# Attention scores of a pair of heads as products of 64 rows in the two row halves of TensorE, with the units' steps in the order of pairs

## The reference, cut to what matters

```python
ql = _rope(_rms_norm(_heads(q, A_HEADS), q_gain), cos, sin)       # A: full attention, 2 kv heads
s = jnp.einsum("bhgqd,bhkd->bhgqk", qi, k) * scale                # 64-wide contraction
p = jax.nn.softmax(s, axis=-1)
return jnp.einsum("bhgqk,bhkd->bhgqd", p, v)
# C: latent keys within +-128 tokens, a sink logit per head in the softmax
# D: all latent keys, a learned bias and a mask on them (4 kv heads)
```

## Time and profile before

| | us |
|---|---|
| median of 3 runs (2863.14 to 2866.6) | 2864.47 |
| the profiled execution | 2871.83 |
| its span in the trace | 2870.0 |
| TensorE busy, all of the span | 2591.3 (90%) |
| VectorE, ScalarE busy | 1084.9 (38%), 585.9 (20%) |

### The profile page before, as it was taken

The page is one execution under the profiler, slowest core; times in us unless marked ns, Lnnn a source line. Parts: engine busy times, 40 slices in busy tenths (PEclk is TensorE's granted clock), DMA queues, the critical chain, the costliest instruction groups (busy, mean ns, idle before and its releaser), DMA issues. The chain is left out here.

```text
span 2870.0 us, 44957 instructions
## 1 busy us (share of the span) xinstructions
PE 2591.3 (90%) x13801; PEld 1283.3 (45%) x13802; DVE 1084.9 (38%) x3199; ACT 585.9 (20%) x1378; POOL 387.1 (13%) x314
## 2 busy tenths in 40 slices
PE   6999989999899999999996588989998989899895
PEld 3566555645433333333332366666553333333331
DVE  3443351534333333333332643451452323233323
ACT  2222341411011111111111341331310111111111
POOL 0000001000021222222221200001001121112122
PEclk9999999999999999999998799999998999999997
DMA  7120303043588998999993402202336999998983
GB/s 272 57 92 30 118 16 136 10 180 125 224 276 305 348 326 281 321 326 327 337 369 101 166 2 91 89 29 103 128 143 252 381 402 387 384 390 277 390 332 110
DMA packets 104980, 619.29 MB, mean 216 GB/s; under 512 B 22832, under 2 KB 23088, under 8 KB 64688
## 3 DMA queue, kind: packets, MB, share of 16 engines
q1 hardware_dynamic: 71184, 530.30, 46.8%
q0 software_dynamic: 33696, 87.63, 12.5%
HBM read 578.84 MB, written 77.99 MB: 229 GB/s over the span
## 5 line engine op out<-in xcount | busy, mean ns | idle before, releaser
L1549 PE MATMUL ps<-wgu,xT 128*64 128x512 f32 x3584 | 808.4, 604 | 49.0 <-DMA wgu<-in_exp_gu 34.8
L1549 PEld LDWEIGHTS ps<-wgu,xT 128*64 128x64 f32 x3584 | 253.1, 139 | 509.2 <-issue 496.6
L1558 PE MATMUL ps<-wd,hiddenT 128*64 128x512 f32 x1824 | 419.5, 602 | 12.7 <-issue 12.2
L1478 POOL DMA_INDIRECT ffn_rows<-Y,six x114 | 182.6, 1602 | 1118.3 <-issue 654.7
L1726 DVE TENSOR_TENSOR hidden<-silu,ps 128x256 f32<-128x256 f32 x112 | 47.2, 421 | 703.9 <-ACT silu L1662 703.9
L659 PE MATMUL ps<-w_in,wgu 128*128 128x512 f32 (+3 forms) x768 | 268.7, 510 | 14.7 <-PEq L609 3.8
L1558 PEld LDWEIGHTS ps<-wd,hiddenT 128*64 128x64 f32 x1824 | 123.4, 137 | 228.3 <-issue 228.3
L659 PEld LDWEIGHTS ps<-w_in,wgu 128*128 128x128 f32 x768 | 151.1, 200 | 124.8 <-issue 111.4
L1662 ACT ACTIVATE silu<-ps 128x256 f32<-128x256 f32 x112 | 43.1, 384 | 800.1 <-PE ps L1549 800.1
L1657 ACT ACTIVATE Y<-ps,wc 128x512 f32<-128x512 f32 x114 | 78.4, 688 | 418.3 <-PE ps L1558 418.3
L1720 DVE TENSOR_SCALAR Y<-ps,wc 128x512 f32<-128x512 f32 x114 | 85.6, 751 | 199.4 <-PE ps L1558 199.4
(11 more groups left out here) (476 smaller groups left out, 2775.9 us busy)
## 6 DMA issues: line engine op xcount, KB each, us to landing
wgu<-in_exp_gu SPq DMA_DIRECT2D x128, 2048.0 KB, 13.9
wd<-in_exp_d SPq DMA_DIRECT2D x128, 1024.0 KB, 13.0
wgu<-in_ada_w SPq DMA_DIRECT2D x40, 1024.0 KB, 4.8
ada_start<-in_ada_w SPq DMA_DIRECT2D x8, 1024.0 KB, 8.0
w_in<-in_w_in SPq DMA_DIRECT2D x4, 2048.0 KB, 10.9
w_in<-in_w_out SPq DMA_DIRECT2D x4, 2048.0 KB, 12.5
wgu<-ffn_rows SPq DMA_DIRECT2D x16, 512.0 KB, 8.3
w_in<-in_w_in SPq DMA_DIRECT2D x2, 3072.0 KB, 14.3
```

The lines of the kernel that those rows point to most:

```text
L1478: pool.indirect_dma_start(out=v.acc_dram, out_offset=bass.IndirectOffsetOnAxis(ap=six[j][:, 0:1], axis=0), in_=Y[j][:, :], in_offset=None, ...
L1549: last = pe.matmul(ps[h * HB:(h + 1) * HB, 0, :], xT[:, k, h * HB:(h + 1) * HB], wgu[w[h]][:, k, :], start=(k == 0), stop=(k == KD - 1))
L1558: last = pe.matmul(ps[h * HB:(h + 1) * HB, 1 + c, :], G[:, f, h * HB:(h + 1) * HB], wd[w[h]][:, f, c * 512:(c + 1) * 512], start=(f == 0), ...
```

## The change

For A, C and D a new `pair_scores(w)` takes the place of `scores(u)`. It computes both units of a pair: for each, only the 64 partitions that hold its head (`rows`) of QT and KT, so the two units' products lie in the two row halves of the array and write to different PSUM buffers. The order is first unit's latent keys, second unit's, first unit's context keys, second unit's. The zeroed half of QT is no longer read, and its two memsets go. `pair_scores(w)` waits until both units of pair w - 1 have their exponentials (`s_exp.wait(pe, 2 * w)`), since both buffers are written again.

All three engines take their steps in pairs for A, C and D; B keeps the old order.

TensorE, the new function and the new order:

```diff
+                def pair_scores(w):
+
+                    s_exp.wait(pe, 2 * w)
+                    a = lo(2 * w)
+                    for c0, c1 in ((a, 512), (512, 768)):
+                        for u in (2 * w, 2 * w + 1) if c1 > c0 else ():
+                            s, q = units[u]
+                            rows = slice(s % 2 * HD, (s % 2 + 1) * HD)
+                            k0 = SEQ if c0 == 512 else key_tile(u, a // P) * P
+                            last = pe.matmul(pp[u % 2][:, c0:c1], QT[rows, s, q * P:(q + 1) * P], KT[rows, s // 2 if isD else 0, k0:k0 + c1 - c0],
+                                             start=True, stop=True)
+                            if c1 == 768:
+                                last.then_inc(s_sc.sem, 1)
...
+                else:
                     s_v.wait(pe, NT)
...
+                    pair_scores(0)
+                    for w in range(NU // 2):
+                        turn_probs(2 * w)
+                        if 2 * w + 2 < NU:
+                            pair_scores(w + 1)
+                        turn_probs(2 * w + 1)
+                        values(w)
```

ScalarE:

```diff
+                else:
+                    exps(1)
+                    for w in range(NU // 2):
+                        probs(2 * w)
+                        if w:
+                            inverse_rows(w - 1)
+                        probs(2 * w + 1)
+                        for u in range(2 * w + 2, min(2 * w + 4, NU)):
+                            exps(u)
```

VectorE:

```diff
-                else:
-                    for side in range(2):
-                        rest = QT[(1 - side) * HD:(2 - side) * HD, :, :].rearrange("p (j s) n -> p j s n", s=2)
-                        dve.memset(rest[:, :, side, :], 0.0).then_inc(s_pad.sem, 1)
...
+                else:
+                    maximum(1)
+                    for w in range(NU // 2):
+                        inverse(2 * w)
+                        context_probs(2 * w)
+                        inverse(2 * w + 1)
+                        if w:
+                            out(w - 1)
+                        if 2 * w + 2 < NU:
+                            maximum(2 * w + 2)
+                        context_probs(2 * w + 1)
+                        if 2 * w + 2 < NU:
+                            maximum(2 * w + 3)
```

More of the change, by code:

```diff
@@ L757, in _ @@
                 s_ke.wait(pe, NT)
-                s_pad.wait(pe, 2)
-                if not isB:
-                    s_v.wait(pe, NT)
[L761 to L768, removed]
+                if isB:
+                    s_pad.wait(pe, 2)
+                    scores(0)
+                    for u in range(NU):
+                        if u + 1 < NU:
+                            scores(u + 1)
+                        if u and u % 2 == 0:
+                            values(u // 2 - 1)
+                        turn_probs(u)
+                    values(NU // 2 - 1)
+                else:
+                    s_v.wait(pe, NT)
+                    pair_scores(0)
[5 more added lines that the diff above has]
+                        values(w)
             @block.scalar
@@ L826, in _ @@
                 exps(0)
[L827 to L834, removed]
+                if isB:
+                    for w in range(NU // 2):
+                        exps(2 * w + 1)
+                        if w:
[3 more added lines that the diff above has]
+                        if 2 * w + 2 < NU:
+                            exps(2 * w + 2)
+                else:
+                    exps(1)
+                    for w in range(NU // 2):
+                        probs(2 * w)
+                        if w:
+                            inverse_rows(w - 1)
+                        probs(2 * w + 1)
+                        for u in range(2 * w + 2, min(2 * w + 4, NU)):
+                            exps(u)
                 inverse_rows(NU // 2 - 1)
@@ L971, in _, with context_probs @@
                     step(dve.tensor_scalar(nsink[:, :], small[:, S_SINK:S_SINK + 4], -1.0, None, ALU.mult))
[L972 to L978, removed]
+                def context_probs(u):
                     s_pt.wait(dve, u + 1)
@@ L981, in _ @@
                     dve.tensor_copy(PT[:, u % 4, 512:768], ps[:, 5 + 2 * (u % 2), 0:256]).then_inc(s_pd.sem, 1)
+                maximum(0)
+                if isB:
+                    for u in range(NU):
+                        if u + 1 < NU:
+                            maximum(u + 1)
+                        inverse(u)
+                        if u and u % 2 == 0:
+                            out(u // 2 - 1)
+                        context_probs(u)
+                else:
+                    maximum(1)
+                    for w in range(NU // 2):
+                        inverse(2 * w)
+                        context_probs(2 * w)
+                        inverse(2 * w + 1)
+                        if w:
+                            out(w - 1)
+                        if 2 * w + 2 < NU:
+                            maximum(2 * w + 2)
+                        context_probs(2 * w + 1)
+                        if 2 * w + 2 < NU:
+                            maximum(2 * w + 3)
                 out(NU // 2 - 1)
@@ L992, in mixer @@
         s_aw[j].stage_over(16 * ((NC + 1 - j) // 2))
-    for s, k in ((s_am, NC), (s_ap, NC), (s_ac, NC), (s_pad, 2), (s_mr, len(runs))):
+    for s, k in ((s_am, NC), (s_ap, NC), (s_ac, NC), (s_pad, 2 if isB else 0), (s_mr, len(runs))):
         s.stage_over(k)
```

## The result

| kernel | median (us) | runs | ratio to before, 95% |
|---|---|---|---|
| before | 2863.80 (2862.64 to 2866.60) | 4 | 1 |
| after | 2885.56 (2885.04 to 2889.74) | 4 | 1.0079 [1.0067, 1.0092] |

The kernel became slower by 21.8 us, where +10.5 was forecast. The direction and the mechanism of the steady pairs were right; the forecast size was half of what came, or less. The first median lies 2.4 us inside the upper end of the stated range (2888) and the second 0.3 us outside it, and both lie above 2883, the highest value that the sum itself gave. That the range held the result is therefore partly luck.

What follows compares the result with a forecast made beforehand. The prediction took A as bound by TensorE, C and D partly by waits. A +1.0 and -0.75, D +4.0 and +2.2, C +2.3 and +1.7 made +10.5 us on the 2864.5 median: 2875, range 2863 to 2888.

Steps and rivals of the forecast that it cites:

- S of a pair with full overlap: Score products of a local pair (latent queries) on TensorE: 1.34 us with row halves overlapping, 2.58 before.
- The wait of V for P: In A, the weighted values wait for ScalarE's copy of the turned exponentials; TensorE idles 0.84 us.
- The last local pair: Last pair with latent queries in a stage, little score work covering waits: 5.3 us; +1.0 in A, +0.7 D, +0.4 C.
- context pairs: Pairs with only context queries, four per layer 0 mixer: 3.15 us against 2.70; +1.75 in A and D, +0.6 in C.
- the two new changes of shape: TensorE's array changes shape four times a pair instead of twice: 0.09 + 0.05 us each, with 0 and 0.25 as ends.
- the loop in D: Exponentials, next pair's scores, maximum, context copy, maximum, exponential: 6.24 us a local pair against 6.12, whatever the scores save.
- Program order inside TensorE: Rival: records start strictly in program order, a pair's scores take 1.71 us; +6 us, 2881; chance 0.13.
- No overlap: Rival: row halves do not overlap, a pair's scores stay at 2.58 us; 2920; chance 0.07.
- Free changes of shape: Rival: changing the array's shape on TensorE costs nothing; about 2865, no difference; chance 0.13.
- TensorE alone sets the pace: Rival: in all three mixers a pair takes 4.7 us; about -50 us, 2815, or 2856 for a part; chance 0.11.
- the terms for the ends of a stage: Stage starts +0.8 us in D, +0.4 in C, -0.15 in A; last local and context pairs priced separately.
- Rival 5: Clock falls in C and D as TensorE idles; 1.2 GHz in half of the pairs: over +60 us, 2930; chance 0.04.

Runs made afterwards that it cites:

- experiment 5: Before's order with each unit's score products made by themselves as products of 64 rows, no zeroed half or memsets: 2909.81 us, 1.0155 of before.
- experiment 4: After's order of pairs, but score products of 128 rows over a zeroed half, with before's memsets: 2921.79 us, 1.0211 of before.
- kernel 7: After with the weighted values made one pair later in A, C and D: 2879.76 us, 1.0058 of before.
- experiment 6: After with all score records of the first unit written ahead of the second's, instead of alternating: 2891.12 us, 1.0096 of before.
- kernel 1: After measured once more (the second median), four remainders written as masks: 2888.32 us, 1.0094 of before.
- kernel 12: Before with nothing changed but four remainders by a power of two written as masks: 2861.08 us, 0.9997 of before.
- kernel 2: After with three products of no use at the start of each stage A, C and D: 2882.39 us, 1.0074 of before.
- kernels 3, 8, 9 and 12: 3: before with fillers at starts, 2866.62 us; 8: row-half pairs with late weighted values in A alone, 2859.64; 9: the same with fillers, 2863.37; kernel 12: own line.

## Why the prediction was right, and where it was short

**Right, within 0.1 us each.** S of a pair with full overlap, 1.34 forecast, with T 1.50 behind the first S. The wait of V for P, 0.84 forecast against 0.83, counted in the same way. A's pair 5.46 against 5.52, D's 6.24 against 6.29. The last local pair 5.3 against 5.33 in A and D, context pairs 3.15 against 3.13. For the two new changes of shape 0.28 was forecast; the rows after show 0.09 (T to S: 0.80 for 0.71) and 0.16 (S to T: 1.50 for 1.34), experiment 5 has 0.18 each. (This list counts steps in A and D; the sum for C was short, see below.) These terms carry the direction, and experiments 4 and 7 show their two causes by themselves: the overlap does save, and what it saves goes into V's wait in A and into the loop in D. With V moved back behind S, A's pair fell to 5.19.

**Rivals.** Program order inside TensorE fell twice (the rows after, experiment 6). No overlap was priced at 2920, and experiment 4, which has none (nor the changes of shape), took 2921.79. Free changes of shape fell in experiment 5. "TensorE alone sets the pace" did not come about even with V late: 5.19 in A and 5.96 in D where it had 4.7. Of the signs that the prediction named for its stages none came: A was to be within 1 us of before, C 2 longer and D 2 to 4 longer, and they are 3.5 and 2.0, 4.6 and 4.6, 6.4 and 5.4 longer. Of the signs of being wrong one came just about: the untouched stretch between C and D of layer 0 moved by 3.1 us.

**Short: the terms for the ends of a stage.** The forecast had A -0.15, C +0.4 and D +0.8 at the starts, 2.1 us over six stages, and nothing behind the last V. Measured, kernel 1 against kernel 12, the starts are longer by 1.79 and 0.91 in A, 1.68 and 1.68 in C, 2.24 and 2.14 in D, together 10.4. The ends behind the last V add 3.6, and C's first steps 1.6 (6.90 and 7.18 for 6.26 at the full clock). That is 8.3 + 3.6 + 1.6 = 13.5 of the 16.1 us by which 26.6 exceeds 10.5. The rest is 0.06 us in each pair of A and D and 0.6 in the local pairs of each C, whose six steps take 5.72 on average at the full clock (5.48 before, 5.63 forecast).

**Its cause.** The waits of the steady pairs were summed right, but the work between the waits at a stage's start and end was priced at 2.4 GHz. Rival 5 asked for the clock in the wrong place: it looked at the pairs of C and D, found it unlikely, and priced half of all pairs. In the steady pairs of after the clock stayed up. It fell at a stage's start, where nothing but S is ready while TensorE waits for the first maximum and exponential, and where after also waits for the second exponential with no S in hand; and at the end, behind the last pair's waits. In A, C and D the stretches at half clock sum to 11.7 us in kernel 12, 58.7 in kernel 1 and 25.0 in kernel 2. Kernel 2 shows that this is the cause in D and in C of layer 1: with work of no use in the gaps no part of these three starts is at half clock, D's is +0.98 over before's and C's +0.79, against +0.8 and +0.4 of the forecast. So the waits themselves were short by 0.2 and 0.4 us, and the clock cost the other 1.26 and 1.15 in D and 0.89 in C. It is not shown for the ends, where no run put fillers. In A of layer 0 fillers gave back 1.18 us, in A of layer 1 and C of layer 0 nothing. With them A's starts have no more time at half clock than before's (2.9 and 3.4 us) and are still 0.6 and 0.9 longer, some of it perhaps the fillers' own time. So A's -0.15 did not come even there, and how much of A's and of layer 0's C is clock stays open.

**A premise that was wrong.** The prediction set its +10.5 on the median because the 7.4 us by which the profiled execution of before lay above it would lie "in no stage that changes". Of the 12.5 us by which that execution exceeds kernel 12's profile, 4.0 lie in stages that change: 3.1 in C and 0.9 in A of layer 0, with the clock down for 11.7 us in that C, which kernels 3, 8, 9 and 12 do not have. This moved no term of the sum, whose rows for the start come from D at full clock. But that C showed, in the profile from which the forecast was made, what a fallen clock costs at a start.

## What to carry to other kernels

When a step gets faster, find the wait that the step used to cover before you count the saving; here V behind S again was worth 0.33 us a pair in A. A loop through two other engines takes from a faster TensorE only what lies in the loop: in D 0.86 of the 1.24 us that S saves (experiment 4). And price the start and the end of a stage by the clock too: a change that takes work out of the gaps there can pay twice, once in waiting and once in slower products after it. A filler helps only where there is a gap to hold it: in A of before there was none, and the start grew by 1.3 to 2.0 us.

## What the hardware showed that was not expected

- Products in the two row halves start independently of the program's order: 13 ns apart with three records between them (7 ns when written alternately), and the pair's S takes 1.56 or 1.57 us in either order.
- With S as products of 64 rows in before's order the clock stayed at 1.2 GHz for all 13.7 us of A's start with TensorE busy for 85% of the time, where the program with products of 128 rows had 3.0 us at that level in a start of 9.1 (kernels 5 and 12). The gap ahead of T is longer there too, so the rows are not shown to be the cause. Fillers of 64 rows failed to hold the clock in four stages and held it in one.
- A clock that falls at the end of a stage stays down in the next: D's projections in layer 0 took 3.1 us more behind after's C, with 6.0 us at half clock.
- Useless products made a kernel faster: 18 of them took 5.9 us off kernel 1, and 24 took 10.5 off kernel 7.
